# Mixer layers: z panels between the state space heads, compression between projection steps, modulation out of the output projection, x in two halves

## The reference

```python
h = rmsnorm(x, attn_norm_w[l])
(z, xbc, dt_raw, sc_b, sc_c, sc_h, q, k_c, v_c, k_s, v_s, k_w, v_w, g_nsa) = split(h @ w_in[l])
y_ssd = ssd_mixer(z, xbc, dt_raw, ...)      # conv + silu on xbc, 8 heads, y * silu(z), rmsnorm
y_sc = sc_b * causal_dwconv(sc_c * sc_h, sc_conv_w[l])
y_nsa = nsa_mixer(q, ...)                   # 4 heads; keys also compressed: gelu(blocks @ w1) @ w2
x = x + concat([y_ssd, y_sc, y_nsa]) @ w_out[l]
```

## Time and profile before

| | us |
|---|---|
| median of 3 runs | 2589.74 (2587.21 to 2590.56) |
| profiled execution, its own time | 2591.64 |
| its span (first to last instruction) | 2589.8 |
| TensorE busy | 2463.4 (95%) |
| VectorE busy | 1719.1 (66%) |
| ScalarE busy | 951.4 (37%) |
| GpSimd busy | 129.0 (5%) |
| mean granted clock of TensorE | 0.971 |

### The profile page before, as it was taken

The page is one execution under the profiler, slowest core; times in us unless marked ns, Lnnn a source line. Parts: engine busy times, 40 slices in busy tenths (PEclk is TensorE's granted clock), DMA queues, the critical chain, the costliest instruction groups (busy, mean ns, idle before and its releaser), DMA issues.

```text
span 2589.8 us, 35848 instructions
## 1 busy us (share of the span) xinstructions
PE 2463.4 (95%) x14588; PEld 2127.0 (82%) x14588; DVE 1719.1 (66%) x2891; ACT 951.4 (37%) x1400; POOL 129.0 (5%) x83
## 2 busy tenths in 40 slices
PE   7988998988999999997899999999999999898998
PEld 6878998868999888886457888888888888677998
DVE  5668876668977976845234795684884845486654
ACT  4555644455644212233233321222321223254332
POOL 0010000010110000010000100001000001001001
PEclk9989999889999999998999999999999999899999
DMA  6324465314454554532110254453454433201543
GB/s 231 139 75 162 169 203 188 133 62 168 176 181 148 204 192 142 185 134 80 49 50 32 82 207 159 139 185 132 143 191 137 171 119 125 98 1 58 187 160 117
DMA packets 66499, 356.92 MB, mean 138 GB/s; under 512 B 7072, under 2 KB 10144, under 8 KB 42016
## 3 DMA queue, kind: packets, MB, share of 16 engines
q1 hardware_dynamic: 66336, 354.65, 39.5%
HBM read 353.57 MB, written 1.05 MB: 137 GB/s over the span
## 4 chain that ended last, share of the span: by engine, by line
PE 76%; DVE 7%; ACT 3%; issue 1%; POOL 0%; DVEq 0%; ACTq 0%; POOLq 0%
PE bank L379 75%; DVE sb_w_lo L1586 2%; ACT sb_w_hi L1044 2%; DVE sb_products L1597 1%; PE bank L1018 1%; DVE sb_rstd L1628 1%; PE bank L933 1%; DVE sb_normed L1674 0%; POOL sb_sq_sum L367 0%; DVE sb_h_lo L1651 0%; DVE sb_mid L1909 0%; ACT sb_rstd L1044 0%; ACT sb_sq L1044 0%; DVE sb_ropet L1908 0%; DVE sb_mid L1721 0%
## 5 line engine op out<-in xcount | busy, mean ns | idle before, releaser
L1586 DVE TENSOR_TENSOR sb_w_lo<-sb_raw,sb_w_hi 128x2048 fp32r<-128x2048 f32 (+1 forms) x281 | 579.3, 2062 | 220.6 <-ACT sb_w_hi L1044 214.9
L1044 ACT ACTIVATE sb_w_hi<-sb_raw 128x2048 fp32r<-128x2048 f32 (+1 forms) x281 | 486.0, 1730 | 377.1 <-PE bank L379 375.2
L379 PE MATMUL bank<-sb_h_hi,sb_w_hi 128*128 128x512 f32 (+1 forms) x1416 | 517.8, 366 | 11.4 <-DVE sb_w_lo L1586 9.6
L379 PE MATMUL bank<-sb_h_lo,sb_w_hi 128*128 128x512 f32 (+1 forms) x1416 | 514.2, 363 | 0.0
L379 PE MATMUL bank<-sb_h_hi,sb_w_lo 128*128 128x512 f32 (+1 forms) x1416 | 514.0, 363 | 0.0
L379 PE MATMUL bank<-sb_hx_hi,sb_w_hi 128*128 128x256 f32 x1632 | 479.4, 294 | 19.7 <-DVE sb_hx_lo L1649 8.2
L379 PE MATMUL bank<-sb_hx_lo,sb_w_hi 128*128 128x256 f32 x1632 | 466.5, 286 | 0.0
L379 PE MATMUL bank<-sb_hx_hi,sb_w_lo 128*128 128x256 f32 x1632 | 466.1, 286 | 0.0
L1597 DVE CUSTOM_DVE_ANT_0 sb_products<-sb_raw,sb_cond,sb_params 128x1024 f32<-128x1024 f32 x288 | 371.8, 1291 | 33.6 <-DVEq L1599 16.5
L379 PE MATMUL bank<-sb_f_hi,sb_w_hi 128*128 128x256 f32 (+1 forms) x1122 | 369.3, 329 | 4.2 <-DVE sb_w_lo L1586 3.9
L379 PE MATMUL bank<-sb_f_hi,sb_w_lo 128*128 128x256 f32 (+1 forms) x1122 | 367.1, 327 | 0.0
(11 more groups left out here) (214 smaller groups left out, 2370.2 us busy)
## 6 DMA issues: line engine op xcount, KB each, us to landing
sb_raw<-w_mod SPq DMA_DIRECT2D x144, 512.0 KB, 3.2
sb_raw<-w_l_up SPq DMA_DIRECT2D x44, 1024.0 KB, 4.8
sb_raw<-w_l_in SPq DMA_DIRECT2D x26, 1024.0 KB, 5.3
sb_raw<-w_l_down SPq DMA_DIRECT2D x32, 704.0 KB, 4.6
sb_raw<-w_m0a_up SPq DMA_DIRECT2D x22, 1024.0 KB, 4.8
sb_raw<-w_m0b_up SPq DMA_DIRECT2D x22, 1024.0 KB, 4.8
sb_raw<-w_m1a_up SPq DMA_DIRECT2D x22, 1024.0 KB, 4.8
sb_raw<-w_m1b_up SPq DMA_DIRECT2D x22, 1024.0 KB, 4.8
```

The costliest lines, as they stand in the source:

```text
L379: return nc.tensor.matmul(out, lhsT, rhs, start=start, stop=stop, skip_group_check=True)
L1044: return nc.scalar.activation(out, in_, func, **kw)
L1586: V.tensor_tensor(w_lo[s][:, 0:w], raw[raw_slot(name, n)][:, 0:w], w_hi[s][:, 0:w].bitcast(F32), ALU.subtract).then_inc(S("raw_free"), 1)
```

## The change

- `IN_ORDER`: the two z panels (11, 12) go from index 8 and 9 to the end. Their steps 184 to 207 stand between the heads, three ahead of each. In the attention stand 32 steps (152 to 183), four to a unit.
- The 16 steps 120 to 135 alternate with two products (four records) of the compression. Its weights stand behind the panel at index 8 in the raw order, behind index 7 before. ScalarE's gelu comes after all eight silus of xbc and, in layer 0, between two of the conditions.
- z is no longer put through silu: ScalarE writes tanh(z/2) and z/2, VectorE makes (tanh + 1) times z/2 ahead of `out`.
- The sc and nsa parts of the output projection's input have buffers of their own (`mix`), and their high halves are made at heads 1 and 2.
- The two modulation chunks of a mixer go from the output projection into the attention (unit 4) and the heads (behind `mats(3)`). VectorE takes `low` of output panel 0 between the last two `mats`, that of panel 1 after the last `out`.
- x arrives in two transfers, the square root's table is loaded ahead of it, all eight squares have buffers of their own, and VectorE adds them.

Cut to its core (buffers and index changes that follow are left out):

```diff
-IN_ORDER = (0, 1, 2, 3, 7, 8, 9, 10, 11, 12, 5, 6, 4)
+IN_ORDER = (0, 1, 2, 3, 7, 8, 9, 10, 5, 6, 4, 11, 12)
...
 _chunk = 0
-for _name, _steps in ([("l0_out", range(2)), ("l0_down", range(0, 16, 2)), ("l1_out", range(2)), ("l1_down", range(0, 8, 2))]
+for _name, _steps in ([("l0_in", IN_ORDER[9:11]), ("l0_down", range(0, 16, 2)), ("l1_in", IN_ORDER[9:11]), ("l1_down", range(0, 8, 2))]
               + [("m0a_up0", range(HALF_FF)), ("m0a_down0", range(4)), ("m0a_up1", range(HALF_FF)),
...
 for _l in range(LAYERS):
-    WHOLE_AFTER[f"l{_l}_in", IN_ORDER[7]] = [(f"l{_l}_cmp", n) for n in range(2)]
+    WHOLE_AFTER[f"l{_l}_in", IN_ORDER[8]] = [(f"l{_l}_cmp", n) for n in range(2)]
 PAIR_W = 1536
...
 def _(sp):
-    sp.dma_start(res[:, :, 0:T], xT).then_inc(S("x_in"), 16)
+    for half in range(2):
+        sp.dma_start(res[:, 4 * half:4 * half + 4, 0:T], xT[:, 4 * half:4 * half + 4, :]).then_inc(S(f"x_in{half}"), 16)
     sp.dma_start(params[:, :], params_d).then_inc(S("params_in"), 16)
...
         mm(bank[5][0:HEADS, T:2 * T], a[:, 1, :], tri[:, 1, :], False, True).then_inc(S("cumulated"), 1)
-        in_steps(88, 112)
+        in_steps(88, 120)
...
             for i in range(CMP_BLOCK // 2):
+                if i % 2 == 0:
+                    in_steps(120 + 8 * c + i // 2, 121 + 8 * c + i // 2)
                 last = mm(bank[6][:, 16 * c:16 * c + N_CMP], w[:, i * P:(i + 1) * P], tpos[:, c, i, :],
...
-        in_steps(112, 120)
-        pe.wait_ge(S("hid_ready"), l + 1)
-        mm(bank[6][:, 64:64 + N_CMP], par(f"k_w2{l}"), hid[:, 0, :], True, True)
-        mm(bank[6][0:N_CMP, 128:192], hid[:, 1, :], par(f"v_w2{l}"), True, True).then_inc(S("cmp_kv"), 1)
-        spread_condition(0)
-        in_steps(120, 136)
-        spread_condition(1)
-        in_steps(136, 148)
-        spread_condition(2)
-
         b = take("att_scores", 8)
...
-        in_steps(148, 152)
-        scores(0)
-        in_steps(152, 160)
-        spread_condition(3)
-
         x = take("xbc_ready", 8)
-        pe.wait_ge(S("xbc_ready"), x + 4)
-        for tb in range(2):
+
+        def turn_x(tb):
+            pe.wait_ge(S("xbc_ready"), x + 4)
             pe.wait_ge(S("in_evac"), e + 9 + tb)
...
-        i = 160
+        def decay_scores(g):
+            pe.wait_ge(S("xbc_ready"), x + 8)
+            pe.wait_ge(S("att_out"), b + 7 + g)
+            B, C = xc[:, 4 + g, :], xc[:, 6 + g, :]
+            mm(bank[6 + g][:, 0:T], B[:, 0:P], C, True, True)
+            mm(bank[6 + g][:, T:384], B[:, P:T], C[:, P:T], True, True).then_inc(S("cb_ready"), 1)
+
+        def fill(a, b):
+            for i in range(a, b):
+                if i in (152, 160):
+                    turn_x((i - 152) // 8)
+                in_steps(i, i + 1)
+
+        spread_condition(0)
+        in_steps(136, 140)
+        spread_condition(1)
+        in_steps(140, 144)
+        pe.wait_ge(S("hid_ready"), l + 1)
+        mm(bank[6][:, 64:64 + N_CMP], par(f"k_w2{l}"), hid[:, 0, :], True, True)
+        mm(bank[6][0:N_CMP, 128:192], hid[:, 1, :], par(f"v_w2{l}"), True, True).then_inc(S("cmp_kv"), 1)
+        spread_condition(2)
+        in_steps(144, 148)
+        scores(0)
+        spread_condition(3)
+        in_steps(148, 152)
+
+        i = 152
         for u in range(8):
...
                 scores(u + 1)
-            fill = (8, 2, 2) if u == 0 else (2, 1, 2) if u < 7 else (2, 2, 2)
-            in_steps(i, i + fill[0])
+            fill(i, i + 2)
             flips(u)
-            in_steps(i + fill[0], i + fill[0] + fill[1])
+            fill(i + 2, i + 3)
             product(u)
-            in_steps(i + fill[0] + fill[1], i + sum(fill))
-            i += sum(fill)
+            fill(i + 3, i + 4)
+            i += 4
...
         spread(1)
-        pe.wait_ge(S("xbc_ready"), x + 8)
-        for g in range(GROUPS):
-            pe.wait_ge(S("in_evac"), e + 12 + g)
-            B, C = xc[:, 4 + g, :], xc[:, 6 + g, :]
-            mm(bank[1 - g][:, 0:T], B[:, 0:P], C, True, True)
-            mm(bank[1 - g][:, T:384], B[:, P:T], C[:, P:T], True, True).then_inc(S("cb_ready"), 1)
-
+        decay_scores(0)
         for hh in range(HEADS):
+            fill(184 + 3 * hh, 187 + 3 * hh)
+            if hh == 0:
+                decay_scores(1)
             if hh + 2 < HEADS:
...
         ws[0] = panel(L + "_out", 0)
+        pe.wait_ge(S("in_evac"), e + 13)
         out_part(0, (4, 5, 6, 7))
...
     pe.wait_ge(S("fills"), 5)
-    norm(KD, T, 1024)
+    pe.wait_ge(S("first_added"), 1)
+    mm(bank[7][:, 0:T], inv[1024][:, :], first_squares[:, 0, :], True, False)
+    mm(bank[7][:, 0:T], inv[1024][:, :], first_squares[:, 1, :], False, True).then_inc(S("norm_sum"), 1)
+    take("rms_done", 1)
     for l in range(LAYERS):
...
                     last = run(tm[:, tb, :], bank[2 + tb][:, 0:TM], ACT.Copy)
+            elif j < 11:
+                last = run(U[:, 2 * n - 2:2 * n, PAD:UW], src, ACT.Copy)
             else:
-                last = run(U[:, 2 * n - 2:2 * n, PAD:UW], src, ACT.Silu if j in (8, 9) else ACT.Copy)
+                run(z_tanh[:, 2 * (j - 11):2 * (j - 11) + 2, :], src, ACT.Tanh, scale=0.5)
+                last = run(U[:, 2 * n - 2:2 * n, PAD:UW], src, ACT.Copy, scale=0.5)
             for t in range(2) if 4 <= j < 8 else ():
...
                 run(ea[:, :], par(f"a_log{l}"), ACT.Exp).then_inc(S("dt_exp"), 1)
-        act.wait_ge(S("raw_free"), RAW_AT[L + "_cmp", 1] + 1 + RAW)
-        run(hid[:, :, :], bank[6][:, 0:32].rearrange("p (c n) -> p c n", c=2)[:, :, 0:N_CMP],
-            ACT.Gelu_apprx_tanh).then_inc(S("hid_ready"), 1)
         for t in range(4):
             silu_xbc(t)
-        condition(0)
         evacuate(7)
         ahead(7)
-        silu_xbc(4)
-        silu_xbc(5)
+        for t in range(4, 8):
+            silu_xbc(t)
+        condition(0)
         condition(1)
+        act.wait_ge(S("raw_free"), RAW_AT[L + "_cmp", 1] + 1 + RAW)
+        run(hid[:, :, :], bank[6][:, 0:32].rearrange("p (c n) -> p c n", c=2)[:, :, 0:N_CMP],
+            ACT.Gelu_apprx_tanh).then_inc(S("hid_ready"), 1)
         evacuate(8)
         ahead(8)
-        silu_xbc(6)
-        silu_xbc(7)
         condition(2)
-        evacuate(9)
         condition(3)
...
         exps(0)
-        ahead(9)
         for u in range(8):
...
             out(u)
-            if u in (1, 4, 7):
-                evacuate(10 + u // 3)
-                ahead(10 + u // 3)
+            if u in (1, 5):
+                evacuate(9 + u // 4)
+                ahead(9 + u // 4)
...
                 ssd_gap(hh + 2)
-            if hh == 1:
+            if hh == 3:
+                evacuate(11)
+                ahead(11)
+            elif hh == 7:
+                evacuate(12)
+            elif hh == 1:
                 act.wait_ge(S("att_out"), b + 8)
                 for i in range(2):
-                    run(h_thin[0][:, 6 + i, :], nsa_y[:, i, :], ACT.Copy).then_inc(S("mix_high"), 1)
-            elif hh == 3:
+                    run(mix[0][:, 2 + i, :], nsa_y[:, i, :], ACT.Copy).then_inc(S("mix_high"), 1)
+            elif hh == 2:
                 for i in range(2):
                     act.wait_ge(S("sc_ready"), 2 * l + i + 1)
-                    run(h_thin[0][:, 4 + i, :], sct[:, i, :], ACT.Copy).then_inc(S("mix_high"), 1)
+                    run(mix[0][:, i, :], sct[:, i, :], ACT.Copy).then_inc(S("mix_high"), 1)
         o = take("ssd_out", 4)
...
         for k in range(4):
+            if k == 2:
+                ahead(12)
             act.wait_ge(S("ssd_out"), o + k + 1)
...
     act.wait_ge(S("fills"), 5)
-    act.wait_ge(S("x_in"), 16)
-    one = square(KD, lambda k: res[:, k, 0:T], T)
-    for k in range(KD - 1):
-        one(k)
+    run(root_warm[:, :], eps[:, :], ACT.Sqrt)
+    for k in range(KD):
+        act.wait_ge(S(f"x_in{k // 4}"), 16)
+        run(first_squares[:, k, :], res[:, k, 0:T], ACT.Square).then_inc(S("first_sq"), 1)
     high("l0_in", 0)
-    one(KD - 1)
+    act.wait_ge(S("norm_sum"), take("norm_sum", 1) + 1)
+    run(rstd[:, 0:T], bank[7][:, 0:T], ACT.Sqrt, bias=eps[:, :]).then_inc(S("rms_done"), 1)
     for l in range(LAYERS):
...
         in_low(8)
+        conv(6)
+        conv(7)
         ck = take("cmp_kv", 1)
...
         if l == 0:
-            conditions(8, 12)
+            conditions(8, 16)
         in_low(9)
-        conv(6)
-        conv(7)
-        if l == 0:
-            conditions(12, 16)
-        in_low(10)
         b = take("att", 8)
...
-        maxes(0)
         xt = take("x_turned", 2)
-        for tb in range(2):
+
+        def scaled_x(tb):
             dve.wait_ge(S("x_turned"), xt + tb + 1)
...
                             ALU.mult).then_inc(S("xdt_ready"), 1)
+
+        maxes(0)
         for u in range(8):
...
             if u == 0:
-                in_low(11)
+                scaled_x(0)
+                in_low(10)
             elif u == 2:
+                scaled_x(1)
+            elif u == 3:
+                in_low(11)
```

(47 more changed lines are left out.)

38 lines of the change are left out of this document (21 added, 17 removed).

## The result

The changed kernel takes 2651.15 us (median of 4 runs, 2646.98 to 2651.46), beside it the kernel before 2590.15 (2587.21 to 2591.97): ratio 1.0233, 95% interval 1.0215 to 1.0251. It is slower, as forecast, but by 61 us and not by 35, and outside the range of 2597 to 2641.

A forecast was written before the change was run, and what follows sets the result against it. The prediction took TensorE as the bound, busy 95% of the span, so a change pays only where it waits or runs at half clock. Its eight terms summed to +35.4 us on 2591.64, less 1.9: 2625, range 2597 to 2641.

The forecast's parts named there:

- Terms 4 to 6: Stages from behind the compression through the heads: +8.7 behind the compression, +3.4 attention, -7.3 heads, in us.
- term 7: Tail from the last output product to the resumed projection: 11.05 us in place of 9.0 and 9.6, cost 3.5.
- 1 start: Start of the kernel: squares need no turn, table loaded before x lands, reciprocal at about 15.0; gain 1.8 us.
- 2 wait ahead of the compression: TensorE waits for the ninth panel's low half before its first compression product: 8.4 and 6.8 us, together +15.2.
- 8 projection and norm: Output projection without chunks: norm starts sooner and at full clock, gain 3.4 and 2.4 us, together 5.8.
- term 3: Compression between steps: 16 rounds of 1.64 us at half clock, 26.2 in each layer, together +19.5 us.
- rival (b): Ninth panel's low half in time, no wait, rounds begin and stay warm at 14.5 us each: 2579; chance 0.07.
- Rival (a): Full clock returns within the rounds: -19 us, so 2606 (2596 to 2614); chance 0.26.
- Term 4 and 5: Late chain behind the compression, +8.7 us, and attention with 32 steps in place of 48, +3.4 us.
- Term 6: Heads with three steps each, taken at full clock, about 2.1 us wait at head 4: gain 7.3 us.
- Rival (c): Clock falls in the new heads too, 4.8 us a head in place of 2.7: 2654; chance 0.07.

The follow-up runs named there:

- warm rounds: Changed kernel with the rounds over steps 128 to 144 and the low halves of the ninth and tenth panels made earlier: 2605.81 us.
- cold entry: As warm rounds, with one line moved back so VectorE makes the ninth panel's low half late again: 2636.6 us.
- new heads: Changed kernel with another order of ScalarE and VectorE in the heads (high half behind exponential 4, chunk's sums split): 2630.6 us.
- thin rounds: As warm rounds, with every second compression product left out: 2592.81 us in a single execution.
- short chain: Changed kernel with warm rounds and new heads, first two condition spreads inside the rounds, third spread and last conditions moved earlier: 2591.03 us.
- short chain with the chunks in the projection: As short chain, with the modulation chunks back in the output projection: 2594.42 us.
- tail order: As new heads, with ScalarE making the second output panel's high half behind the norm's last two squares: 2640.1 us.
- chunk in two units: As short chain, with the attention chunk's two sums in the fifth and sixth unit instead of both in the fifth: 2592.79 us.

## Why the prediction went wrong

The step that failed is the clock behind the waits. The prediction foresaw the waits behind the rounds and at head 4 and added up their lengths, but took the attention and the heads themselves at full clock (for the heads in so many words: "I take full"). The runs showed half clock behind those waits: 20.5 us of it in layer 0's attention, 6.8 and 13.7 us in the heads. Terms 4 to 6 came out 18.3 us higher than forecast, of 23.7 us that were missing in all. The tail (term 7, 5.4 us) was added up wrongly and left out a table load and more than half of GpSimd's last sum; the window attention, 4.9 us, is in no term; the rounds were priced 4.7 us too high, which hid as much of the loss.

Against its terms, in us over both layers, worked out from the starts of TensorE's records in the two profiles:

| term | forecast | measured |
|---|---|---|
| 1 start | -1.8 | -2.2 |
| 2 wait ahead of the compression | +15.2 | +15.0 |
| 3 rounds | +19.5 | +14.8 |
| 4, 5 behind the rounds to the heads | +12.1 | +21.6 |
| 6 heads | -7.3 | +1.5 |
| 7 tail to the resumed projection | +3.5 | +8.9 |
| 8 projection and norm | -5.8 | -5.4 |
| window attention, untouched | 0 | +4.9 |

They sum to 59.1 of 59.6. A step counts 0.36 wherever it was moved. The table ends the old heads of layer 1 0.35 us earlier than the prediction (20.30 against 20.65 us); by the prediction's boundary terms 6 and 7 would be +1.1 and +9.2.

**Right.** The start (20.29 to 18.12). The wait that "decides the case": 8.27 and 6.70 us against 8.4 and 6.8, worked out from VectorE's back-to-back rows alone. Half clock throughout the rounds; a cold round is 0.78 for the step and 0.71 for four records, 1.49 us and not 1.64: a record among steps takes 0.18 and not the 0.21 of the earlier trace rows. That is the 4.7. The wait for the tenth panel in layer 1, 2.59 against 2.8. The projection: the norm waits 1.16 us in place of 2.85, a little over the "under 1", and the first step of the up projection follows 3.2 and 2.2 us sooner, against 3.4 and 2.4.

**Right outcome, wrong reason, in term 3.** The prediction gave as grounds that a round is dense for only 0.4 of its time, so that the rounds would not win the clock back, and it priced rival (b) as if they could also keep it; that they do both is now measured. Sixteen rounds with no wait ahead take 12.8 us with their first step (rival (b) had 14.5), behind the waits of the changed kernel 23.9. Rival (a), the clock returning within them, happened in none of the runs with cold rounds. What the prediction booked as two costs, wait and mixing, was one: between warm rounds and cold entry, 9.5 us of waits moved 30.8 us. So half throughout was right because of the wait, and not because the rounds are thin.

**Term 4 and 5, +9.5.** Nearly all of it is in layer 0 (15.9 measured against 7.6; layer 1 has 5.7 against 4.5). The waits were foreseen as such (gelu, conditions, tenth panel), their order of size too. Left out was what follows them: after four waits of 0.87 to 1.86 us the clock is at half for 20.5 us more of the attention, which the prediction had at 1.00. The new heads show the size of it: the same code behind the rounds took 63.7 us there with 14.3 us of half clock in all and 68.4 us here with 25.7, so 20.5 us of it are worth some 8.6 (an estimate from these two), against 8.3 missing. Why the clock falls in one profile and not in the next stays open: of the four with this code, three have one stretch of 10.2 us in the attention and this one has two; and no run ties the half clock here to the length of a wait (thin rounds, short chain and short chain with the chunks in the projection). And a unit with four steps was priced at 4.9 us; it takes 5.15 at full clock, against 5.27 with five in the kernel before (two units from 113.48 to 124.02). TensorE isn't what sets the pace there, so steps taken out of it save little: 0.25 x 8 = 2 us a layer, which smaller waits elsewhere made good in layer 1.

**Term 6, +8.8.** A head at full clock takes 2.68 us, as priced (2.7). The wait at head 4 is 2.92 against 2.1, and part of what it was ascribed to is wrong: not the chunk but only ScalarE's z and high half ahead of exponential 4, then the first output that must leave its bank; ScalarE in layer 0:

```profile
182.35 1.09 ACT L1063 ACTIVATE sb_mid<-bank 128x512 f32<-128x512 f32 x2
183.31 1.93 ACT L1063 ACTIVATE sb_w_hi<-sb_raw 128x2048 fp32r<-128x2048 f32 x1
185.11 0.54 ACT L1063 ACTIVATE sb_decays<-sb_decays 128x384 f32<-128x384 f32 x1
```

Larger is the half clock with that wait, 6.8 us in layer 0 and 13.7 in layer 1, 10.2 of them from the wait on. The prediction names it ("if that happens here, up to +2 a layer") from the earlier trace rows and then takes full. The new heads show the price of wait and half clock together: 24.67 us with neither, for 28.36 and 30.89. Rival (c), a clock at half throughout the heads, did not occur.

**Term 7, +5.4.** From the last output product to the resumed projection 14.0 and 13.8 us against a forecast of 11.05. The forecast does not come out of its own parts: those that it lists up to the root make 8.4 us, with the 3.85 from the reciprocal on 12.25. The rows of layer 0 show the rest:

```profile
198.30 1.28 ACT L1063 ACT_TABLE_LOAD   x1
202.26 2.29 DVE L1612 TENSOR_TENSOR sb_w_lo<-sb_raw,sb_w_hi 128x2048 fp32r<-128x2048 f32 x1 [0.74 <-ACT sb_w_hi L1063]
202.60 2.53 POOL L372 TENSOR_TENSOR sb_sq_sum<-sb_sq,sb_sq_sum 128x256 f32<-128x256 f32 x1 [1.36 <-ACT sb_sq L1063]
```

The path is ScalarE's: z's evacuation, then a table load that the list doesn't have, two squares, the high half, a square; VectorE's gates and outputs run beside it. Then GpSimd's last sum takes 2.53 us and not 1.0. It runs beside VectorE's low half; in the kernel before, with no low half beside it, it takes 0.92, and in the tail order, with the low half later, the last two take 1.61 together. That VectorE slows it is what these rows suggest; no run isolates it. Last, the norm's products and the root take 2.6 and 2.4 us for 1.6. The tail order shows that moving the high half behind the squares costs more than it wins; of the two places tried, the one in the change is the better.

**The last +4.9** is in no part of the change. Between two norms near the end stands the window attention, the same code in all kernels. It takes 195.4 us in the kernel before with 20.5 us of half clock in it, and 200.3 in the changed one with 30.7. Windows of 110 us about it, the kernel before and the changed one:

```profile
2235.00:2345.00 110.00, 99.88 (x552) 73.09 (x551) 85.39 (x287) 50.74 (x123) 0.00 (x0) 0.91 0.06 20
```

```profile
2290.00:2400.00 110.00, 99.34 (x522) 72.45 (x522) 81.21 (x272) 48.00 (x116) 0.00 (x0) 0.86 0.06 20
```

Over all profiles the stage took 194.5 to 195.4 us with 20.5 us of half clock, 198.1 with 27.3, and 200.2 to 200.3 with 30.7 or 34.1. The short chain took 200.3 us and the chunk in two units 195.4, though they reach it 0.9 us apart. Why, no run settles. A difference of up to 5 us in this kernel can come from there.

## What to carry to other kernels

Thin work between dense steps kept full clock where TensorE came to it without a wait, and never won it back behind a wait of 2.39 us or more. So before moving such work, make sure that the operand of its first product is ready when TensorE gets there, and price such a wait not at its length but at its length plus half clock up to the next long dense stretch. Where shorter waits stand in a stage of mixed work, as in the attention here, allow for half clock as a range: the same code had 10 us of it in one profile and 20 in another. Where a moved wait is foreseen, look for the one line of another engine's order that removes it. A stage paced by other engines (here the attention) holds dense steps cheaply (0.23 us for a step of 0.36), so taking them out saves little.

## What the runs showed of the hardware

The rounds hold 0.50 for 22.89 us without any gap in TensorE's work, and 1.00 for 12.30 us with the same products in the same order; a wait ahead of them, of 2.39 us in the shortest case, decided for half. So busy time alone did not release the clock. The Trainium skill, page "TensorE: Matmul & The Clock Gate", section "Part 1: The HAM clock gate (the "warmup" mystery)", says that sustained activity releases the throttle and advises against idle gaps between bursts. The advice holds in these runs (the gap was worth 30.8 us); that sustained work releases the clock again does not, for rounds of this kind.

Heads with three steps ahead of each held 1.00 over 24.67 us in both layers of the new heads, where the kernel before, with none, has 0.67 and 0.66. With the wait of 2.92 us at head 4 the same heads have 0.88 and 0.78.

A tanh between exponentials needs no table load: none stands in ScalarE's rows of the changed kernel between the exponential at 180.28 and the one at 185.11, with z's tanh at 182.35 between them. This agrees with the Trainium skill, page "ScalarE: Activation LUTs", section "Table sets: the hidden batching unit".
